# Branch outputs in three fp32r terms, whole residual-gate tiles, and a new dealing of the adaLN tiles in a trunk layer's gate stage

## The reference, cut to what matters

```
mod = c @ ada_w + ada_b; sh1, sc1, gt1, sh2, sc2, gt2 = split(mod, 6)
h = modulate(rmsnorm(x, norm1_g), sh1, sc1)
u = h @ w_in                                # 2048 -> 3584 + 4*2048
y_a = pool_mixer(u_A) ; y_b = conformer_conv(u_B) @ conf_w_out
y_c = short_conv(u_C) @ sc_w_out ; y_d = fourier_mixer(u_D) @ fnet_w_out
gates = sigmoid(u_G).reshape(b, s, 4, 2048)
merged = sum_k gates[k] * y_k
x = x + gt1 * (merged @ w_o)
h2 = modulate(rmsnorm(x, norm2_g), sh2, sc2)
x = x + gt2 * hier_moe(h2, ...)             # 32 experts, 2 per token
return rmsnorm(x, final_g)
```

## Time and profile before

| | |
|---|---|
| runs | 1850.55, 1845.27, 1842.77 us; median 1845.27 |
| profiled execution | 1846.03 us, of it 1844.2 us between first and last instruction |
| mean granted TensorE clock | 0.984 of full speed |
| busy: PE, PEld, DVE, ACT | 95%, 55%, 49%, 21% |
| read from memory | 639 MB, 348 GB/s over the span |
| packets on SyncE's queue | 87.2% of the 16 engines' time |

### The profile page before, as it was taken

One profiled execution on the slowest core, in us unless ns is written; L12 is line 12 of the kernel. 1 busy time (PEld: TensorE's weight loads), 2 busy tenths in 40 slices (PEclk: granted clock), 3 DMA queues, 4 the chain that ended last, 5 costly groups with the idle time before them and its releaser, 6 DMA issues.

```text
span 1844.2 us, 26118 instructions
## 1 busy us (share of the span) xinstructions
PE 1759.1 (95%) x10273; PEld 1009.7 (55%) x10274; DVE 899.9 (49%) x1046; ACT 392.4 (21%) x476; POOL 0.8 (0%) x5
## 2 busy tenths in 40 slices
PE   2999999999999988899999999999999999999996
PEld 2888557876777766686444444444444444434342
DVE  4564958866677566556433332323333232333334
ACT  3001034322233222234110111101011110101111
POOL 0000000000000000000000000000000000000000
PEclk8999999999999999899999999999999999999998
DMA  9997539988779577655799999999999999999995
GB/s 370 387 363 294 182 137 337 336 323 327 272 277 377 210 264 284 240 186 225 294 422 422 422 422 423 421 422 422 422 423 421 423 421 422 422 422 422 422 423 219
DMA packets 139758, 641.93 MB, mean 348 GB/s; under 512 B 9283, under 2 KB 9411, under 8 KB 81475
## 3 DMA queue, kind: packets, MB, share of 16 engines
q1 hardware_dynamic: 139282, 639.18, 87.2%
q0 software_dynamic: 144, 1.70, 0.2%
q10 hardware_dynamic: 290, 0.46, 0.1%
HBM read 639.21 MB, written 2.10 MB: 348 GB/s over the span
## 4 chain that ended last, share of the span: by engine, by line
PE 73%; DMA 22%; DVE 3%; ACT 1%; issue 1%; SPq 0%; DVEq 0%; ACTq 0%
PE ps L924 18%; DMA ring<-in_exp_w 15%; PE ps L578 8%; PE ps L888 8%; DMA ring<-in_ada_w 7%; PE ps L672 5%; PE ps L674 5%; PE ps L673 5%; PE ps L911 4%; PE ps L635 4%; PE ps L866 4%; PE ps L591 3%; PE ps L752 2%; PE ps L753 2%; PE ps L754 2%; DVE r_m L1418 1%
## 5 line engine op out<-in xcount | busy, mean ns | idle before, releaser
L924 PE MATMUL ps<-ring 128*64 128x512 f32 x2048 | 464.7, 596 | 4.1 <-DMA ring<-in_exp_w 4.1
L924 PEld LDWEIGHTS ps<-ring 128*64 128x64 f32 x2048 | 143.0, 137 | 289.7 <-issue 289.6
L1658 DVE TENSOR_TENSOR r_h<-r_h,ps 128x1024 f32<-128x1024 f32 x124 | 145.9, 1218 | 203.5 <-PE ps L911 203.5
L673 PE MATMUL ps<-g_lo,h_hi 128*128 128x512 f32 x512 | 202.4, 395 | 0.0
L1631 DVE TENSOR_TENSOR r_c<-ps,scale 128x512 f32<-128x512 f32 x65 | 44.7, 688 | 294.5 <-PE ps L866 293.6
L672 PE MATMUL ps<-mix_hi,h_hi 128*128 128x512 f32 x384 | 158.7, 413 | 10.6 <-DVE g_lo L1384 10.6
L1201 ACT ACTIVATE r_m<-ps 128x512 f32<-128x512 f32 x32 | 19.1, 597 | 697.4 <-PE ps L924 697.4
L1081 ACT ACTIVATE mix_hi<-ring 128x1024 fp32r<-128x1024 f32 x96 | 101.5, 1061 | 243.6 <-PE ps L674 243.6
L674 PE MATMUL ps<-mix_hi,h_lo 128*128 128x512 f32 x384 | 151.1, 393 | 0.0
L578 PE MATMUL ps<-r_h,ring 128*128 128x256 f32 x640 | 141.3, 384 | 5.0 <-ACT r_h L1031 5.0
L1384 DVE TENSOR_TENSOR g_lo<-ring,mix_hi 128x1024 fp32r<-128x1024 f32 x96 | 117.0, 1225 | 56.5 <-ACT mix_hi L1081 54.7
(11 more groups left out here) (266 smaller groups left out, 1658.4 us busy)
## 6 DMA issues: line engine op xcount, KB each, us to landing
ring<-in_exp_w SPq DMA_DIRECT2D x320, 1024.0 KB, 19.7
ring<-in_w_in SPq DMA_DIRECT2D x36, 2048.0 KB, 10.1
ring<-in_ada_w SPq DMA_DIRECT2D x70, 1024.0 KB, 8.3
r_b<-in_exp_w SPq DMA_DIRECT2D x64, 1024.0 KB, 20.8
ring<-in_w_in SPq DMA_DIRECT2D x20, 1024.0 KB, 14.2
ring<-in_ada_w SPq DMA_DIRECT2D x32, 512.0 KB, 4.3
ring<-in_w_o SPq DMA_DIRECT2D x8, 2048.0 KB, 8.8
ring<-in_branch_w SPq DMA_DIRECT2D x6, 2048.0 KB, 8.4
```

Of the source, the lines that this page charges most:

```text
L673: mm(ps[:, b + t, :], h, lo[:, cols], start=False, stop=False)
L924: last = mm(ps[m * NWIN:(m + 1) * NWIN, 2, :], xe[:, k, :], chunk(2 * c + m)[:, kk * F:(kk + 1) * F], start=(k == 0), stop=(k == KT - 1))
L1658: V.tensor_tensor(x1n, x1n, ps[:, (6, 4)[b]:(6, 4)[b] + 2, :].rearrange("p b n -> p (b n)"), ALU.add).then_inc(added, 1)
```

## The change: what it does

1. **Branch outputs.** For the wide branches the output becomes three fp32r products per fp32 product. The branch `brT[g]` is split once, into a high part (ACT, `branch_high`, after piece 2's copy of unit j=0) and a low part in place (DVE, after piece 3's). The output weights are split per unit in four slices k of 128 x 512: `branch_w_high` on ACT into three buffers, `branch_w_low` on DVE in place in slot BW, for k = 0 to 2 behind the gate pieces i = 5 to 7, for k = 3 behind the sigmoid, once TensorE is done with k = 0. TensorE goes through k outermost and waits for each k's low part.
2. **Residual-gate tiles.** The GT1 tiles come whole, 128 x 2048, through two buffers: the upper half of slot ADA and `r_b[:, 1024:3072]`, free by then. Their bias row is loaded behind the first two.
3. **Dealing.** `TILE_AT[g][j]` says after which gate piece (END: after the last low part of the output weights) DVE takes a tile, and `TILE_ISSUE[g]` which tiles SyncE's groups issue. Branch 0 has four per unit (after pieces 0, 2, 4 and at END); branches 1 and 2 have 2, 5, 5 and 4; branch 3 has 1, 5, 5 and 5. No tile stands at pieces 5 to 7.
4. **Head.** `head_sums(part + 1)` is issued within the last unit of a part, before its slices 2 and 3, and the second `add_part` comes before slice 12 in place of 8.
5. **Order on ACT.** The first three gate pieces are copied before the DFT result, the fourth right behind it. ACT's loop over the branches is written out.
6. `ct` is cut in two tiles (`ct`, `n_win`); what is computed from them is the same. New semaphores go with the new buffers.

```diff
+        br_r = at("br_r", [P, N_BRANCH, MT, S], F32R, (N_SLOT + 1) * SLOT * 4)
+        bw_lo = at("bw_lo", [P, 4, 2 * MIX], F32R, BW * SLOT * 4)
+        bw_pair = at("bw_pair", [P, 2, MIX], F32R, 147456 + 7168 * 4)
+        bw_third = sb("bw_third", [P, MIX], F32R)
+        bw_hi = [bw_pair[:, 0, :], bw_pair[:, 1, :], bw_third[:, :]]
+
+        def br_high(g):
+            return br_r[:, (g - 1) % 2, :, :]
...
+        END = 8
+        TILE_AT = [[(0, 2, 4, END)] * 4, [(4, END), (0, 2, 3, 4, END), (0, 2, 3, 4, END), (0, 2, 4, END)],
+                   [(4, END), (0, 2, 3, 4, END), (0, 2, 3, 4, END), (0, 2, 4, END)],
+                   [(END,), (0, 2, 3, 4, END), (0, 2, 3, 4, END), (0, 2, 3, 4, END)]]
+        TILE_ISSUE = [(0, 2, 4, 6, 8, 10, 12, 14, 16), (0, 2, 3, 5, 8, 10, 13, 15, 16),
+                      (0, 2, 3, 5, 8, 10, 13, 15, 16), (0, 2, 2, 4, 7, 9, 12, 14, 16)]
+
+        def tile_buffer(g, k):
+
+            if g < N_BRANCH - 1:
+                return slot(ADA)[:, k % 2 * D:(k % 2 + 1) * D]
+            return r_b[:, 1024:3072] if k % 2 else slot(ADA)[:, 2048:4096]
...
-            def ada_tiles(g, k, n):
-
-                vec = SH2 + g
-                for i in range(n):
-                    sp.wait_ge(acc_step, ADA1 + 16 * g + max(k + i - 1, 0))
-                    sp.dma_start(slot(ADA)[:, i % 2 * D:(i % 2 + 1) * D], ada_v[:, k + i, vec * D:(vec + 1) * D]
-                                 ).then_inc(ada_tile[i % 2], 16)
-
-            def gt1_tile(k, half):
-
-                if k:
-                    sp.wait_ge(acc_step, ADA2 + 2 * (k - 1) + half + 1)
-                else:
-                    sp.wait_ge(acc_step, ADA2)
-                sp.dma_start(slot(ADA)[:, 2048 + half * 1024:3072 + half * 1024],
-                             ada_v[:, k, GT1 * D + half * 1024:GT1 * D + (half + 1) * 1024]).then_inc(ada_tile[half], 16)
+            def ada_tile_in(g, k):
+
+                vec = SH2 + g if g < N_BRANCH - 1 else GT1
+                sp.wait_ge(acc_step, ADA1 + 16 * g + max(k - 1, 0))
+                sp.dma_start(tile_buffer(g, k), ada_v[:, k, vec * D:(vec + 1) * D]).then_inc(ada_tile[k % 2], 16)
...
-                        if g < N_BRANCH - 1:
-                            ada_tiles(g, 4 * j + 2 * i, 2)
-                        else:
-                            if j == 0 and i == 0:
-                                sp.wait_ge(acc_zero, 1)
-                                sp.dma_start(acc[0:1, :], gt1_bias).then_inc(bias_in, 16)
-                            if j == 3:
-                                load_wo(i)
-                            first = (0, 1, 2, 4, 6, 8, 11, 13, 16)
-                            for k in range(first[2 * j + i], first[2 * j + i + 1]):
-                                for half in range(2):
-                                    gt1_tile(k, half)
+                        if g == N_BRANCH - 1 and j == 3:
+                            load_wo(i)
+                        for k in range(TILE_ISSUE[g][2 * j + i], TILE_ISSUE[g][2 * j + i + 1]):
+                            ada_tile_in(g, k)
+                        if g == N_BRANCH - 1 and j == 0 and i == 0:
+                            sp.wait_ge(acc_zero, 1)
+                            sp.dma_start(acc[0:1, :], gt1_bias).then_inc(bias_in, 16)
...
-                head_sums(part)
...
+                        if n == ORDER[part][-1] and kk == 2 and part < 3:
+                            head_sums(part + 1)
...
-                    if j % 2 == 0:
-                        pe.wait_ge(bw_in, 16 * (2 * (g - 1) + j // 2 + 2))
                     pe.wait_ge(y_saved, 4 * g + j - 1)
                     if g == N_BRANCH - 1 and j >= 2:
                         pe.wait_ge(m_parts, j - 1)
                     if j == 0:
                         pe.wait_ge(mod_ready, 4 + g)
-                    last = gate_y(n, MT, lambda k, t: brT[:, g, k, t * P:(t + 1) * P],
-                                  lambda k: bw[:, k, (j % 2) * MIX:(j % 2 + 1) * MIX])
-                    last.then_inc(y_done, 1)
+                        pe.wait_ge(br_parts, g)
+                    for k in range(MT):
+                        pe.wait_ge(bw_lo_done, 16 * (g - 1) + 4 * j + k + 1)
+                        hi, lo = bw_hi[k % 3], bw_lo[:, k, (j % 2) * MIX:(j % 2 + 1) * MIX]
+                        for t in range(TT):
+                            toks = slice(t * P, (t + 1) * P)
+                            mm(ps[:, y_bank(n) + t, :], br_high(g)[:, k, toks], hi, start=(k == 0), stop=False)
+                            mm(ps[:, y_bank(n) + t, :], br_high(g)[:, k, toks], lo, start=False, stop=False)
+                            last = mm(ps[:, y_bank(n) + t, :], br_r[:, g, k, toks], hi, start=False, stop=(k == MT - 1))
+                        last.then_inc(bw_used if k < 3 else y_done, 1)
...
-            act.wait_ge(dft_done, 5)
-            A(r_b[:, 3072:4096], ps[:, 2:4, :], ACT.Copy).then_inc(dft_saved, 1)
+            def branch_high(g):
+
+                act.wait_ge(y_done, 4 * g)
+                act.wait_ge(conf_ready, MT)
+                A(br_high(g), brT[:, g, :, :], ACT.Copy).then_inc(br_hi_done, 1)
+
+            def branch_w_high(g, j, k):
+
+                if k == 0 and j % 2 == 0:
+                    act.wait_ge(bw_in, 16 * (2 * (g - 1) + j // 2 + 2))
+                if k == 3:
+                    act.wait_ge(bw_used, 12 * (g - 1) + 3 * j + 1)
+                else:
+                    act.wait_ge(y_done, 4 * g + j)
+                A(bw_hi[k % 3], slot(BW)[:, k * 1024 + (j % 2) * MIX:k * 1024 + (j % 2 + 1) * MIX], ACT.Copy
+                  ).then_inc(bw_hi_done, 1)
...
+                        if 32 * g + x == AHEAD:
+                            continue
                         if x < 32 or not last:
                             gate_high(g, x)
                         else:
                             wo_high(x - 32)
+                        i = x - 8 * j - AHEAD
+                        if g and j == 0 and i == 2:
+                            branch_high(g)
+                        if g and i >= 5:
+                            branch_w_high(g, j, i - 5)
...
+                    if g:
+                        branch_w_high(g, j, 3)
...
             for x in range(AHEAD):
                 gate_high(0, x)
+            act.wait_ge(dft_done, 5)
+            A(r_b[:, 3072:4096], ps[:, 2:4, :], ACT.Copy).then_inc(dft_saved, 1)
+            gate_high(0, AHEAD)
...
-            gate(0, False)
-            with act.Fori(1, N_BRANCH - 1) as g:
+            for g in range(N_BRANCH - 1):
...
-                    if part and k in (0, 8):
-                        add_part(part - 1, 3 + k // 8)
+                    if part and k in (0, 12):
+                        add_part(part - 1, 3 + k // 12)
...
-                if j == 0 and i >= 4:
-                    ada_one(g, i - 4)
-                elif j > 0 and i % 2 == 1:
-                    ada_one(g, 4 * j + i // 2)
+                if i in TILE_AT[g][j]:
+                    ada_one(g, sum(len(u) for u in TILE_AT[g][:j]) + TILE_AT[g][j].index(i))
...
-                    if i % 2 == 1:
-                        ada_one(0, 4 * j + i // 2)
+                    ada_step(0, j, i)
+                ada_step(0, j, END)
...
-            def gt1_piece(k, half):
-
-                v.wait_ge(ada_tile[half], 3 * 128 + 16 * (k + 1))
-                v.wait_ge(bias_in, 16)
-                cols = acc[:, half * 1024:(half + 1) * 1024]
-                V.scalar_tensor_tensor(out=cols, in0=slot(ADA)[:, 2048 + half * 1024:3072 + half * 1024],
-                                       scalar=ccol[:, k:k + 1], in1=cols, op0=ALU.mult, op1=ALU.add
-                                       ).then_inc(acc_step, 1)
-                v.wait_ge(acc_step, ADA2 + 2 * k + half + 1)
+
+            def branch_w_low(g, j, k):
+
+                v.wait_ge(bw_hi_done, 16 * (g - 1) + 4 * j + k + 1)
+                V.tensor_tensor(bw_lo[:, k, (j % 2) * MIX:(j % 2 + 1) * MIX],
+                                slot(BW)[:, k * 1024 + (j % 2) * MIX:k * 1024 + (j % 2 + 1) * MIX],
+                                bw_hi[k % 3].bitcast(F32), ALU.subtract).then_inc(bw_lo_done, 1)
...
-                        if last:
-                            begin = (0 if j == 0 else 10 * j - 8) + (max(i - 6, 0) if j == 0 else i + i // 4)
-                            size = (i >= 6) if j == 0 else 1 + (i % 4 == 3)
-                            for h in range(begin, begin + size):
-                                gt1_piece(h // 2, h % 2)
-                        else:
-                            ada_step(g, j, i)
+                        ada_step(g, j, i)
+                        if j == 0 and i == 3:
+                            v.wait_ge(br_hi_done, g)
+                            V.tensor_tensor(br_r[:, g, :, :], brT[:, g, :, :], br_high(g).bitcast(F32), ALU.subtract
+                                            ).then_inc(br_parts, 1)
```

(14 more changed lines are left out.)

24 lines of the change are left out of this document (13 added, 11 removed).

## The result

The changed kernel takes 1818.8 us (median of 4 runs, 1815.2 to 1819.8) against 1845.4 us before (4 runs beside it): ratio 0.985, 95% interval 0.982 to 0.988. The forecast was 1812, with a range of 1798 to 1829. So the gain is 26.6 us where 33.6 were expected. In the profiled executions the span went from 1844.2 to 1817.9 us, 26.3 less.

What follows compares the result with a forecast made beforehand. TensorE was taken to bound the part ahead of the routing table, the expert weights the end. Gains 3.8 + 4.8 + 17.2 + 25.8 less 18 for new waits made 33.6 us, so 1812 us, range 1798 to 1829.

Steps and rivals of the forecast that it cites:

- A: Head sums: moved half a unit ahead of the part's end, they hide TensorE's 1.25 us idle at three changes: 3.8 us.
- B: First gate pieces split ahead of the DFT copy: TensorE's wait before the first gate product shrinks, worth 4.8 us.
- C: Branch outputs: twelve times 16 fp32 records in 6.87 us become 24 fp32r products in 5.44 us, worth 17.2 us.
- D: TensorE's waits for adaLN tiles in branches 1 to 3 go, with whole tiles in two buffers: 25.8 us.
- E: New TensorE waits at branch outputs, as late tiles hold VectorE's output low parts: 18 us lost, bounds 3 and 32.
- T: The moment at which the outputs of the unit before are done; later times in a unit count from it.
- the stream's T+17.4: Lower case for j=2: the queue drains in stream, seven MB are there at T+17.4, and nothing is lost.
- Half clock: TensorE products at half clock after the new j=2 waits: 1.6 us each, 3 us in all.
- 1 (no new waits, 1797): Tiles land in stream and VectorE's 1 us spare per unit suffices: gain 48.6, 1797 us; chance 0.15.
- 2 (branch 3 keeps its waits): SyncE's gate loads still stand behind branch 3's tiles: gain 16.5, 1829 us; chance 0.12.
- 3 (two buffers are a cycle): Each tile waits until the one two before is consumed, so five-tile units run over: slower, 1855 us; chance 0.04.
- 4 (C is 0): Three terms at the clock's lower level or splits too late in every unit: 1829 us; chance 0.04.

Runs made afterwards that it cites:

- Experiment 4: Kernel before with only the head's part (sums within the last unit, second addition before slice 12) and ACT's order: 1835.5 us, ratio 0.994.
- experiment 1: Changed kernel, but in units with five tiles SyncE issues the tile for piece 4 ahead of the gate (or w_o) weights: 1800.5 us, ratio 0.976.
- experiment 5: On top of experiment 1, one of the five tiles of unit j=2 moved to j=0 in branches 1 and 2: 1795.5 us, ratio 0.973.
- experiment 6: On top of experiment 1, the first tile of j=2 issued ahead of the output weights in branches 1 to 3: 1795.2 us, ratio 0.973.
- Experiment 7: The edits of experiment 5 and experiment 6 together: 1793.9 us, ratio 0.972.
- experiment 8: Kernel before with only branch 3's GT1 in 16 whole tiles through two buffers, dealt 1, 5, 5, 5: 1821.1 us, ratio 0.988.
- experiment 3: Changed kernel with the tiles of branches 1 and 2 at their places of before and issued two by two: 1823.2 us, ratio 0.989.
- experiment 9: Experiment 7 with the branch outputs as fp32 products again, without splits: 1808.5 us, ratio 0.980.

## Why the prediction was right or wrong

*The mechanism* was right for A to D, and for E in what makes TensorE wait, but one step of E was not, and the time is 6.8 us off, nearly all of it in that term. Of the signs that the prediction named, A's and B's came, C's nearly (5.48 for 5.4), and E's three waits of 3 to 5 us came (3.76, 3.58, 3.41), with four more that this sign didn't name; the second half's length changed by under 0.1 us. D's sign did not come: VectorE waits up to 3.89 us for tiles in branch 3. And branch 3's unit j=2 takes 32.5 us, over the 32 that it set as a sign of being wrong: 8 of the 23.1 us that D took from branch 3 come back there in E (1.5, 4.35 and 2.15).

*A and B*: right; 3.6 and 5.0 against 3.8 and 4.8. Experiment 4 has them alone, at 9.5 with 8.6 expected. (In A, 1.84 and 3.5 give 5.3 and not 5.1; nothing hangs on it.) *C*: right at its size, 16.8 against 17.2. The forecast took the pitch from the row and not from four passes becoming three, and the row was right: 24 products take 5.48 us, not 5.15. *D*: right as a wait of the gate pieces, 25.8; its branch-3 part alone, 23.1, gave 24.5 by the medians and 22.7 in the traces.

*E* was mis-sized, 24.9 in place of 18. By its parts:
- j=2, waits and steps: 4.7, 4.5 and 4.35 against 4, 4 and 3.5. Nearly right. That tile landed at about T+21, as the row for T+22 had said; the stream's T+17.4 and the estimate of T+18.8 by the Trainium skill (DMA: Bandwidth & Descriptors, Anatomy of one DMA) were both too early here. Neither allowed for SyncE's wait: in branch 1 the tile was issued only at T+13.3, when its buffer was free, and landed 8.0 us after that.
- j=1: 2.4, 2.4 and 1.5 against 0.7, 0.7 and 0.6. This is the largest error, 4.3 us. The step "in j=1 the like tile has 2 MB ahead only" took the bytes in front for the lateness. But that tile is issued only at T+10.8, when its buffer is free, lands 8.2 us after that, at T+19.0, and VectorE wants it at T+15.6. In experiment 1 the same tile, issued before the gate weights, landed 4.9 us after its issue.
- Of this, 0.8 each is the step within the output. It was counted in the price of j=2 only, and comes wherever the first low part is late: five times by itself, and twice under the half clock.
- j=3 of branch 3: 2.15 against 1.
- Half clock: 3.0 beyond the 0.8 already counted in each of those two outputs (2.05 and 0.95), as forecast in sum, but by luck: it came after two of the three long waits and not, as priced, after all three. The 0.5 ahead of the gate row did not come.
- VectorE's own time with the 128x512 form: 0.68 to 0.69 us with a pitch of 0.60, as taken (0.69 and 0.62).

Two of these came from one habit. I priced the tile that comes *last* with care and gave the others of the same pattern a fraction by analogy. All seven units have a tile wanted at piece 4 and issued behind 2 MB; one row, the wait at that tile, should have been sought in each of them.

*The rivals.* 1 (no new waits, 1797): its end is about where the change could have gone with another order, and experiments 5 to 7 are there at 1794 to 1796. It didn't come by itself. 2 (branch 3 keeps its waits): no, and experiment 8 shows the opposite, though 8 us of them are back as waits of the outputs. 3 (two buffers are a cycle): the time says no. In the seven units a tile took 10.3 us at most from issue to landing; two elsewhere took 13.1 and 12.1 and held up nobody. 4 (C is 0): taken literally no, the products are as fast as said. But as a net effect it was closer than its chance of 0.04: with fp32 outputs the changed kernel is *faster*. C and E are not two terms but one edit and its price, and the sum 17.2 - 18 stood in my own working. I didn't draw the conclusion that the three terms would bring nothing as dealt.

## What to carry to other kernels

When an engine with work to spare gets a new duty that the bound engine waits for, look at what stands ahead of that duty in its in-order stream, and at where the transfers for those instructions stand in *their* queue: VectorE was busy 51% of the span here, but 25 of 28.9 us in such a unit, and TensorE waited for it seven times. The busy share of the stage is the one to read, not that of the page. A load that is wanted in the middle of a unit goes ahead of the large load that is wanted in the next one; that exchange, without a byte or an instruction more, was worth 18 us by the medians and 15 in the gate stage. And an edit that shortens the bound engine's work also takes away the cover under which others caught up, so its price is to be worked out together with its gain.

## What the runs showed of the hardware

The w_o stage has the same three waits in every kernel's profile (1.11, about 1.94 and 2.41 us), yet TensorE's clock fell after both of the longer ones in six of the eleven profiles (those of the kernel before and of the changed one among them), after the last alone in three (experiments 3, 5 and 8), and after neither in two (experiments 1 and 6). The same two waits in the changed kernel and in experiment 6:

```profile
738.86 0.50 PE L770 MATMUL ps<-pad_hi,m_hi 128*128 128x512 f32 x1 [1.93 <-DVE g_lo L1503]
740.29 0.63 PE L772 MATMUL ps<-pad_hi,m_lo 128*128 128x512 f32 x1
815.26 0.79 PE L770 MATMUL ps<-mix_hi,m_hi 128*128 128x512 f32 x1 [2.41 <-DVE g_lo L1503]
```

```profile
718.28 0.50 PE L773 MATMUL ps<-pad_hi,m_hi 128*128 128x512 f32 x1 [1.93 <-DVE g_lo L1506]
793.05 0.50 PE L773 MATMUL ps<-mix_hi,m_hi 128*128 128x512 f32 x1 [2.41 <-DVE g_lo L1506]
```

In the first, products of 0.63 us (the 1.2 GHz level) follow each of the two longer waits, and the granted clock is 0.96 in the 40 us from 731 and again from 811, which is 1.6 us lost each time; in the second it is 1.00 in all four such stretches from 711 to 871. From the start of w_o to the end there are 1086.3 us in the first and 1081.4 in the second: 4.9 us with no difference in the work there, of which the clock's rows explain 3.2. Over the eleven profiles this part takes 1084.4 to 1086.7 us with both drops and 1081.4 and 1082.0 with none. Experiment 7 has the early part 2.8 us shorter than experiment 6 (w_o at 708.29 against 711.06) and the later one 4.9 us longer, so its profiled span is the longer one, 1794.6 against 1792.5, though its median is lower. A single span can mislead by this much.

The first head part shows the same at its start. The same 144 products come after the same wait of 1.31 us, and take 32.6 us in experiments 6 and 9 and 34.2 in experiment 7, with a granted clock of 0.83, 0.82 and 0.64 from 41.4 to 50 us and 1.00 from there to 76. The Trainium skill (TensorE: Matmul & The Clock Gate, What's actually happening) says that the monitor behind the clock runs free of the program, so that one kernel has more or fewer slow products at its start from run to run. The first head part agrees with it; the drops that came after the same waits in some profiles only would fit it too, but no run here isolates their cause.

A tile's time in the queue depended on what had been issued just before it: the same 1 MB took 4.9 us from issue to use in experiment 1, and 8.2 us in the changed kernel, 4.3 us behind 2 MB. In the kernel before, tiles of 0.5 MB took from 3.6 to 13.4 us.
